# Gate and up units of both feed-forward blocks as seven half-width block products, a first part kept as it was

## What is computed

```
h = h + 0.5 * swiglu(rmsnorm_2(h, ffn1_norm), ffn1_w_gate, ffn1_w_up, ffn1_w_down)     # 528 tokens
... latent attention and delta net ...
h = h + 0.5 * swiglu(rmsnorm_2(h, ffn2_norm), ffn2_w_gate, ffn2_w_up, ffn2_w_down)     # only 512 are needed
def swiglu(x, w_gate, w_up, w_down): return (silu(x @ w_gate) * (x @ w_up)) @ w_down   # 1024 -> 2816 -> 1024
```

## Time and profile before

| | |
|---|---|
| median of 3 runs | 2112.35 us (2111.82 to 2117.05) |
| span of the profiled execution | 2111.5 us; the profile gives no time beside the span |
| block 1 (window 797 to 1178.9) | from its unit 1 to the last down product |
| block 2 (window 1740 to 2098.3) | the same |
| TensorE busy | 2059.4 us, 98% |
| Vector, Scalar, GpSimd busy | 817.3, 736.1, 761.0 us |

### The profile page before, as it was taken

One profiled execution on the slowest core, in us unless ns is written; L12 is line 12 of the kernel. 1 busy time (PEld: TensorE's weight loads), 2 busy tenths in 40 slices (PEclk: granted clock), 3 DMA queues, 4 the chain that ended last, 5 costly groups with the idle time before them and its releaser, 6 DMA issues.

```text
span 2111.5 us, 32172 instructions
## 1 busy us (share of the span) xinstructions
PE 2059.4 (98%) x13992; PEld 1769.5 (84%) x13992; DVE 817.3 (39%) x1300; ACT 736.1 (35%) x1140; POOL 761.0 (36%) x243
## 2 busy tenths in 40 slices
PE   8999999999999999999999999999999999999998
PEld 6899888878977789999999878798777788888886
DVE  4400675145357655220222242266566644211222
ACT  5332222336556544221222344342312323222222
POOL 4433232545310054334333431045243235434432
PEclk9999999999999999999999999999999999999999
DMA  5323122222310122223323431222013223223322
GB/s 173 100 87 109 52 74 80 80 90 81 100 61 21 41 80 81 81 75 106 100 66 94 103 100 31 60 68 81 22 62 111 81 82 98 90 83 107 100 68 72
DMA packets 170052, 171.52 MB, mean 81 GB/s; under 512 B 16940, under 2 KB 160680, under 8 KB 169912
## 3 DMA queue, kind: packets, MB, share of 16 engines
q1 hardware_dynamic: 168508, 167.25, 25.1%
q10 hardware_dynamic: 1404, 2.23, 0.3%
HBM read 163.17 MB, written 6.29 MB: 80 GB/s over the span
## 4 chain that ended last, share of the span: by engine, by line
PE 89%; DVE 4%; issue 3%; ACT 2%; POOL 1%; DMA 1%; ACTq 0%; SPq 0%; DVEq 0%; POOLq 0%
PE ps L2101 87%; PE ps L2103 2%; DMA x_rows<-in_x 0%; ACT diag L927 0%; DVE gdn_x L1966 0%; DVE gdn_inv_t L1949 0%; POOL w_lo L758 0%; POOL stat L775 0%; ACT u_hi L953 0%; DMA ret_decay<-c_decay 0%; ACT w_hi L899 0%; ACT residual L952 0%; DVE gdn_inv_t L1945 0%; DVE tmp L1414 0%; DVE sg L1609 0%
## 5 line engine op out<-in xcount | busy, mean ns | idle before, releaser
L758 POOL TENSOR_TENSOR w_lo<-w_raw,w_hi 128x2048 fp32r<-128x2048 f32 (+3 forms) x153 | 654.8, 4282 | 901.7 <-ACT w_hi L899 896.2
L2101 PE MATMUL ps<-u_hi,w_hi 128*128 128x512 f32 (+1 forms) x1904 | 584.4, 347 | 9.8 <-DVE sg L1609 2.6
L2101 PE MATMUL ps<-u_hi,w_lo 128*128 128x512 f32 (+1 forms) x1904 | 578.6, 344 | 0.0
L2101 PE MATMUL ps<-u_lo,w_hi 128*128 128x512 f32 (+1 forms) x1904 | 569.5, 344 | 1.0 <-DVE u_lo L1402 0.8
L2101 PEld LDWEIGHTS ps<-u_hi,w_hi 128*128 128x128 f32 x1904 | 328.6, 189 | 53.0 <-issue 5.5
L2101 PEld LDWEIGHTS ps<-u_lo,w_hi 128*128 128x128 f32 x1904 | 326.6, 189 | 43.7 <-DVE u_lo L1402 5.5
L2101 PEld LDWEIGHTS ps<-u_hi,w_lo 128*128 128x128 f32 x1904 | 328.1, 189 | 40.0 <-issue 0.5
L899 ACT ACTIVATE w_hi<-w_raw 128x2048 fp32r<-128x2048 f32 (+3 forms) x157 | 279.0, 1779 | 175.0 <-PE ps L2101 168.9
L2101 PE MATMUL ps<-hidden_hi,w_hi 128*128 128x264 f32 (+1 forms) x528 | 141.1, 321 | 0.0
L2101 PE MATMUL ps<-hidden_lo,w_hi 128*128 128x264 f32 (+1 forms) x528 | 141.0, 322 | 0.0
L2101 PE MATMUL ps<-hidden_hi,w_lo 128*128 128x264 f32 (+1 forms) x528 | 140.8, 321 | 0.0
(11 more groups left out here) (379 smaller groups left out, 2959.8 us busy)
## 6 DMA issues: line engine op xcount, KB each, us to landing
w_raw<-in_w_in_a SPq DMA_DIRECT2D x22, 1024.0 KB, 5.3
w_raw<-in_ffn_w_gate SPq DMA_DIRECT2D x22, 1024.0 KB, 5.4
w_raw<-in_ffn_w_up SPq DMA_DIRECT2D x22, 1024.0 KB, 5.4
w_raw<-in_w_in SPq DMA_DIRECT2D x17, 1024.0 KB, 5.2
w_raw<-in_ffn_w_down SPq DMA_DIRECT2D x16, 768.0 KB, 4.2
w_raw<-in_ffn_w_down SPq DMA_DIRECT2D x16, 640.0 KB, 3.9
w_raw<-in_w_out_a SPq DMA_DIRECT2D x8, 1024.0 KB, 5.0
w_raw<-in_w_kv SPq DMA_DIRECT2D x8, 1024.0 KB, 5.4
```

Source lines behind the costliest of these rows:

```text
L758: pool.tensor_tensor(WL[:, u % RAWS, part], RAW[:, u % RAWS, part], WH[:, u % SPLITS, part].bitcast(F32), ALU.subtract).then_inc(lo_done, 1)
L2101: return nc.tensor.matmul(o, a, b, start=start, stop=stop, **kw)
```

## The change

FFN_PARTS becomes (4, 6, 6, 6), and each part's down product has 4 units that hold all of the part's rows. The 4 gate and up units of the first part are computed as before. The 18 of the others are computed in blocks. Write a unit's weights as a 2 x 2 of blocks (4 row blocks of 128 by 128 columns, b11 to b22) and the input as a 2 x 2 (4 feature blocks by half of the tokens). Seven products p1 to p7 of blocks or of sums of blocks, 12 matmuls of 264 or 256 columns each, give the four output blocks. TensorE adds where it can: a product is accumulated into a bank that already holds another, seeded by a Scalar copy from bank to bank (y from p1, w from y behind p6), while p5 is copied to SBUF and added by Vector to y and, from w, to z. The banks: x, w are slot s0, y, z slot s1; at the end x|w and y|z are the two output chunks.

- The input is normalised once per block: Vector makes `normed` (8 operations of width 528 or 512) behind unit 0, its three sums behind unit 1, their low parts behind units 2 and 3; Scalar makes the high parts. During the first two down units u_hi and u_lo are rewritten from `normed`. Silu then reads PSUM directly.
- Weights: Vector makes four sums of 512 elements (one in place in RAW), and the low part of the first 1024 elements and of the 1536 of the sums; Scalar makes the high parts in three pieces; GpSimd makes the low part of the last 1024 only.
- All this is done one unit ahead, between the pieces for the current unit. The first unit of a part's sevens is prepared in the third down unit before it.
- For the first two seven-product units of each block TensorE starts banks y and w with one matmul each before the Scalar seeds.

The core of the diff (indentation cut by 8):

```diff
-FFN_PARTS = (12, 10)
+FFN_PARTS = (4, 6, 6, 6)
+ORDER = ("p1", "p5", "p6", "p2", "p7", "p3", "p4")
...
-    ffns[name] = [(job(part, spread_after=3 if name == "ffn1" and part == FFN_PARTS[0] else None),
-                   job(8, fold=2, kc=part // 2)) for part in FFN_PARTS]
+    ffns[name] = [(job(part, spread_after=3 if name == "ffn1" and n == 0 else None), job(4, kc=part))
+                  for n, part in enumerate(FFN_PARTS)]
...
+        if u in seven_no:
+            v = seven_no[u]
+            pool.wait_ge(w_summed, 4 * v + 4)
+            pool.wait_ge(sum_lo, 2 * v + 1)
+            lo_part(u, slice(UNIT // 2, UNIT), u + 2)
+        elif u < n_units:
...
+        if u + 1 in seven_no and u not in seven_no:
+            return
+        if u + 2 in seven_no:
+            first_rows_hi(u + 2)
+            last_rows_hi(u + 2)
+            summed_hi(u + 2)
+        else:
+            hi(u + 2)
...
+    def first_rows_hi(u):
+        v = seven_no[u]
+        a, b, half = u % RAWS, u % SPLITS, UNIT // 2
+        act.wait_ge(done, unit_ticks[u - SPLITS])
+        act.wait_ge(w_summed, 4 * v + 2)
+        nc.scalar.activation(WH[:, b, 0:half], RAW[:, a, 0:half], ACT.Copy).then_inc(sum_hi, 1)
+    def last_rows_hi(u):
+        hi_part(u, slice(UNIT // 2, UNIT), raw_in[u % RAWS])
+    def summed_hi(u):
+        v = seven_no[u]
+        if v >= 2:
+            act.wait_ge(done, unit_ticks[seven_units[v - 2]])
+        if u in first_sevens:
+            act.wait_ge(mixed, 10 * first_sevens.index(u) + 10)
+        act.wait_ge(w_summed, 4 * v + 4)
+        nc.scalar.activation(TH[:, v % 2, :], TF[:, v % 2, :], ACT.Copy).then_inc(sum_hi, 1)
...
+        def seven_unit(jg, i, j):
+            u = jg.unit0 + 4 * i + j
+            v = seven_no[u]
...
+            x, y, z, w = 2 * s0, 2 * s1, 2 * s1 + 1, 2 * s0 + 1
+            act.wait_ge(prod, product_tick(u, "p1"))
+            nc.scalar.activation(PS[:, y, 0:half], PS[:, x, 0:half], ACT.Copy).then_inc(seeded, 1)
+            act.wait_ge(prod, product_tick(u, "p5"))
+            if v:
+                act.wait_ge(added, 2 * v)
+            nc.scalar.activation(P5[:, 0:half], PS[:, z, 0:half], ACT.Copy).then_inc(seeded, 1)
+            if u + 1 in seven_no:
+                first_rows_hi(u + 1)
+            act.wait_ge(prod, product_tick(u, "p6"))
+            nc.scalar.activation(PS[:, w, 0:half], PS[:, y, 0:half], ACT.Copy).then_inc(seeded, 1)
+            if u + 1 in seven_no:
+                last_rows_hi(u + 1)
+                summed_hi(u + 1)
+            if u + 2 not in seven_no:
+                hi(u + 2)
+            for m in (1, 0):
+                slot, uses = slots[m]
+                if j % 2 == 0:
+                    if m:
+                        act.wait_ge(prod, product_tick(u, "p3"))
+                        act.wait_ge(added, 2 * v + 2)
+                    else:
+                        act.wait_ge(done, unit_ticks[u])
+                    nc.scalar.activation(SG[:, m, 0:width].rearrange("p (a n) -> p a n", a=2),
+                                         PS[:, 2 * slot:2 * slot + 2, 0:half], ACT.Silu).then_inc(ps_free[slot], 1)
+                else:
+                    act.wait_ge(ps_free[slot], uses + 1)
+                    nc.scalar.activation(HH[:, 4 * i + 2 * (j // 2) + m, 0:width], TMP[:, m, 0:width], ACT.Copy).then_inc(hh_done, 1)
...
+    def w_sums(u):
+        if u not in seven_no:
+            return
+        v = seven_no[u]
+        e, a = v % 2, u % RAWS
...
+        dve.wait_ge(raw_in[a], 16 * (u // RAWS + 1) + 16 * extra_loads(u))
+        if v >= 2:
+            dve.wait_ge(done, unit_ticks[seven_units[v - 2]])
+        nc.vector.tensor_tensor(t3, b12, b22, ALU.subtract).then_inc(w_summed, 1)
+        dve.wait_ge(w_summed, 4 * v + 1)
+        nc.vector.tensor_tensor(b12, b12, b11, ALU.subtract).then_inc(w_summed, 1)
+        dve.wait_ge(w_summed, 4 * v + 2)
+        nc.vector.tensor_tensor(t2, b12, b22, ALU.subtract).then_inc(w_summed, 1)
+        dve.wait_ge(w_summed, 4 * v + 3)
+        nc.vector.tensor_tensor(t4, b21, t2, ALU.add).then_inc(w_summed, 1)
+    def first_rows_lo(u):
+        v = seven_no[u]
+        a, b, half = u % RAWS, u % SPLITS, UNIT // 2
+        dve.wait_ge(sum_hi, 2 * v + 1)
+        dve.wait_ge(w_summed, 4 * v + 3)
+        nc.vector.tensor_tensor(WL[:, a, 0:half], RAW[:, a, 0:half], WH[:, b, 0:half].bitcast(F32),
+                                ALU.subtract).then_inc(sum_lo, 1)
+    def summed_lo(u):
+        v = seven_no[u]
+        dve.wait_ge(sum_hi, 2 * v + 2)
+        nc.vector.tensor_tensor(TL[:, v % 2, :], TF[:, v % 2, :], TH[:, v % 2, :].bitcast(F32),
+                                ALU.subtract).then_inc(sum_lo, 1)
...
+    def normalise(name, number):
         cols = norms[name][1]
         width = width_of(cols)
+        for k in range(KC):
+            last = nc.vector.scalar_tensor_tensor(out=UN[:, k, 0:width], in0=RES[:, k, cols], scalar=gain(name, k),
+                                                  in1=RSTDB[:, 0:width], op0=ALU.mult, op1=ALU.mult)
+        last.then_inc(mixed, 1)
...
+        dve.wait_ge(mixed, 10 * number + 1)
+        nc.vector.tensor_tensor(s3, a21, a11, ALU.subtract).then_inc(mixed, 1)
+        dve.wait_ge(mixed, 10 * number + 2)
+        nc.vector.tensor_tensor(a21, a21, a22, ALU.add).then_inc(mixed, 1)
+        dve.wait_ge(mixed, 10 * number + 3)
+        nc.vector.tensor_tensor(s2, a11, a21, ALU.subtract).then_inc(mixed, 1)
+        dve.wait_ge(mixed, 10 * number + 4)
+        nc.vector.tensor_tensor(s4, a12, s2, ALU.add).then_inc(mixed, 1)
...
+            if j == 0:
+                normalise(name, number)
+            if j == 1:
+                mix_sums(name, number)
+            if j == 2:
+                mix_low(1, 1)
+                mix_low(0, 2)
+            if j == 3:
+                mix_low(2, 3)
...
+        def seven_unit(part, jg, i, j):
+            u = jg.unit0 + 4 * i + j
+            v = seven_no[u]
+            slots = [chunk_of(jg, i, j, m) for m in range(2)]
+            (s0, uses0), (s1, uses1) = slots
+            y, z, w = [PS[:, b, 0:half] for b in (2 * s1, 2 * s1 + 1, 2 * s0 + 1)]
+            up = j % 2
+            def hidden_out(m):
+                slot, uses = slots[m]
+                gate_slot, gate_uses = chunk_of(jg, i, j - 1, m)
+                dve.wait_ge(ps_free[gate_slot], gate_uses + 1)
+                nc.vector.tensor_tensor(TMP[:, m, 0:width].rearrange("p (a n) -> p a n", a=2),
+                                        SG[:, m, 0:width].rearrange("p (a n) -> p a n", a=2),
+                                        PS[:, 2 * slot:2 * slot + 2, 0:half], ALU.mult).then_inc(ps_free[slot], 1)
+            w_sums(u + 1)
+            dve.wait_ge(prod, product_tick(u, "p6"))
+            dve.wait_ge(seeded, 3 * v + 3)
+            nc.vector.tensor_tensor(y, P5[:, 0:half], y, ALU.add).then_inc(added, 1)
+            if u + 1 in seven_no:
+                first_rows_lo(u + 1)
+            dve.wait_ge(prod, product_tick(u, "p7"))
+            nc.vector.tensor_tensor(z, P5[:, 0:half], w, ALU.add).then_inc(added, 1)
+            if up:
+                dve.wait_ge(prod, product_tick(u, "p3"))
+                dve.wait_ge(added, 2 * v + 2)
+                hidden_out(1)
+            elif (i, j) != (0, 0):
+                tile = 2 * i + j // 2 - 1
+                for m in range(2):
+                    hidden_low(part, tile, m, 2 * tile + 2)
+            if u + 1 in seven_no:
+                summed_lo(u + 1)
+            if up:
+                dve.wait_ge(done, unit_ticks[u])
+                hidden_out(0)
...
+                if part == 0 and j < 2:
+                    rows = slice(k4 * j, k4 * (j + 1))
+                    dve.wait_ge(mix_hi, 5 * number + 4 + j)
+                    nc.vector.tensor_tensor(UL[:, rows, cols], UN[:, rows, 0:width], UH[:, rows, cols].bitcast(F32),
+                                            ALU.subtract).then_inc(mixed, 1)
...
+    def seven(name, number, jb, n, cols):
+        i, j = n // 4, n % 4
+        u = jb.unit0 + n
+        v, half, k4 = seven_no[u], width_of(cols) // 2, KC // 2
+        a, b, e = u % RAWS, u % SPLITS, v % 2
+        (s0, uses0), (s1, uses1) = [chunk_of(jb, i, j, m) for m in range(2)]
+        x, y, z, w = 2 * s0, 2 * s1, 2 * s1 + 1, 2 * s0 + 1
+        low, high = slice(cols.start, cols.start + half), slice(cols.start + half, cols.stop)
...
+        made = {"p1": (own(0, 0), plain(0, low), x, True), "p5": (own(0, 1), plain(0, high), z, True),
+                "p6": (summed(0), mixed_in(0), y, False), "p2": (own(1, 0), plain(k4, low), x, False),
+                "p7": (summed(1), mixed_in(1), w, False), "p3": (own(1, 1), mixed_in(2), y, False),
+                "p4": (summed(2), plain(k4, high), w, False)}
+        for name in ORDER:
+            if name == "p1":
+                pe.wait_ge(sum_lo, 2 * v + 1)
+                if u in first_sevens:
```

(77 more changed lines are left out.)

187 lines of the change are left out of this document (123 added, 64 removed).

## The result

The changed kernel takes 2090.53 us (median of 4 runs, 2087.86 to 2090.91); the kernel before took 2114.7 beside it (4 runs). The ratio is 0.9883, 95% interval 0.9867 to 0.9899: faster by 1.2%. The forecast was 2096.5 with its own range from 2086 to 2107. The profiled execution spans 2088.5 us against 2111.5.

The account below looks back on a forecast made before the run. TensorE, busy 98% of the span, was taken as the bound, so matmul columns set the cost. Terms of -21.5 and +5.6 for the clock took 2111.5 to a 2095.6 span, median 2096.5; own range 2086 to 2107, with rivals 2072 to 2113.

Parts of the forecast that it names:

- The columns, -47.5: Gate and up units of both blocks: 84 half-width matmuls instead of 96 in 18 units each, 47.5 us less.
- The last seven-product unit, +13.8: Last such unit per part: GpSimd's split delays Vector's sums' low part, p6 waits 2.2 or 2.4, six times, +13.8 us.
- Twelve short waits, +2.4: Gate units behind up units: Scalar's seed ready at 3.0, p6 wants it at 2.9; 0.2 each, +2.4 us.
- Block 1's first part, +4.4: Vector's eight normalising operations after unit 0 delay unit 2's second chunk: +4.4 us, 0 to 9.
- Block 2's first part, +4.2: Normalising plus GpSimd splits make a hidden low part late for the first down product: +4.2 us, 0 to 7.
- Clock, +5.6: Eight new waits in dense feed-forward work may lower TensorE's granted clock, 0.7 us each: +5.6 us.
- Rival A: The port does not stop Vector long, or Scalar's copy comes 1.5 later: 2074 us, chance 0.12.
- Rival B: Vector is the bound in every unit, 11.1 us a unit: 2109 us, chance 0.12.
- Rival C: The clock falls after each wait of p6 and of the first parts: slower, 2122 us, chance 0.12.
- First sums, low parts and rewriting in the first down units, 0: Block 1's first down units: 25.9 us of Vector work against 23.5 of down units, costing 0, up to 2.
- start matmuls: Matmuls into two banks for four units, 8 of 264 or 256 columns: +1.0 us.

Follow-up runs that it names:

- e6: Changed kernel with e2's order, plus normalise behind unit 1 and all three low parts of the input sums behind unit 3: 2067.01 us, 0.9782.
- e2: Changed kernel with Vector making the low part of the next unit's weight sums ahead of the hidden low parts in gate units: 2075.41 us, 0.982.
- e5: Changed kernel with Scalar's high part of the coming down unit later only in a part's second last seven-product unit: 2075.93 us, 0.9825.
- e7: Changed kernel with GpSimd's 1536-element low part of a down unit split into three instructions of 512: 2084.1 us, 0.9863.
- e8: e2 with two more Vector sums of 384 elements in every preparation of a seven-product unit: 2075.47 us, 0.9824.
- e1: Changed kernel with Scalar's high part of the coming down unit later in both last seven-product units of a part: 2121.56 us, 1.0038.
- e4: Kernel before with parts (4, 6, 6, 6) and undivided down units, all gate and up units full products: 2114.36 us, 0.9999.
- e3: Changed kernel with Vector's normalising moved from behind unit 0 to behind unit 1's hidden low parts: 2090.28 us, 0.9885.

## Why the prediction was right, and where it was off

- **The columns, -47.5.** Right. e6 has no new wait in the blocks; its span is 48.1 us shorter than before, of which 1.6 are clock loss (6.1 - 4.5). That leaves 46.5, where 47.5 - 1.0 were booked. In the changed kernel two units together take 20.55 us in block 1 (p6 starts at 888.74 and 909.29) and 19.87 in block 2 (1799.70 and 1819.57), where twice 10.28 and twice 9.95 were booked.
- **The last seven-product unit, +13.8.** Right in place, number and size: six waits, 13.0 in all, 2.0 and 2.3 where 2.2 and 2.4 were forecast. The walk gave 13.1 us from the start of the gate unit to the end of GpSimd's split, 13.7 to the end of the second hidden low part and 15.5 to that of the sums' low part. That unit starts at 906.35 (worked out in the next item), and the three end at 919.47, 920.03 and 921.71: 13.1, 13.7 and 15.4. The mechanism is shown by three separate edits. Doing the wanted operation first (e2) and letting the split loose later (e5) remove the waits whole; shorter pieces (e7) halve them. By the Trainium skill, "SBUF — State Buffer", section "Who interferes with whom", the loser is blocked for the whole instruction. The trace agrees: in e5 GpSimd takes 4.29 instead of 3.51 when Vector came first. That the two take turns when both queue stands on e7.
- **Twelve short waits, +2.4.** Wrong: none appears. The rows of one such unit of block 1:

```profile
887.58 0.65 ACT L1242 ACTIVATE hidden_hi<-tmp 128x528 fp32r<-128x528 f32 x1 [1.63 <-DVE tmp L1885]
888.13 0.38 ACT L1216 ACTIVATE ps<-ps 128x264 f32<-128x264 f32 x1
...
888.74 0.28 PE L2353 MATMUL ps<-mix_hi,w_sum_hi 128*128 128x264 f32 x1
```

TensorE starts p6 at 888.74, so the unit began 24 matmuls of 0.1224 earlier, at 885.80. (The next gate unit, which the item above uses, begins two units later, 20.55, at 906.35.) Scalar begins the seed at 888.13 and ends it at 888.51, 2.7 after the unit's start, not 3.0. Instructions on one engine begin up to 0.1 before the one ahead has ended, and over the chain that saved 0.3 us, more than the whole term. In all twelve units the seed is ready 0.16 to 0.24 us early; the waits were missed by that much. With more work for Vector (e8) three of them do appear.
- **Block 1's first part, +4.4.** Measured 2.0. Two terms were off. Eight normalising operations take 5.52 back to back, not 6.1, for the same overlap. And the clock fell at 808 to 812, ahead of any new wait; it slowed TensorE by some 1.7 us, so that it came late by itself. Where the fall comes later, as in e1 and e8, the same wait is 3.5. So the small 2.0 is luck in part: e4 has the fall at 808 as well, without the change in the products.
- **Block 2's first part, +4.2.** Measured 2.8, at the first down unit as forecast. The normalising with one split inside took 9.77 us where 10.7 (6.1 and 4.6) were booked, and the rest of a walk of 30 us was another half a microsecond too long. The row of the normalising:

```profile
1735.68 9.77 DVE L1809 SCALAR_TENSOR_TENSOR normed<-residual,gains,rstd_row 128x512 f32<-128x512 f32 x8
```

e6 shows that only the order made these waits. e3 shows that half the order is not enough.
- **Clock, +5.6.** The sum is close (11.2 - 6.1 = 5.1), by luck in part. Eight waits were measured, and two of them, at 1763.9 and 1841.9, had a low clock behind them, some 1.7 us each: 3.4. The other 1.7 is what is left of falls that stand behind no new wait: two came, at 808 and 1644, and the one at 722 went away. The forecast wanted a low clock only behind the new waits, and that is wrong. The fall at 808 begins as the wait of 1.6 us that the kernel before has too ends, and e4 trades 722 for 808 in the same way. What makes a fall come at 722, 808 or 824 in one kernel or another, and at 1644, stays open.
- **Rival A** (the port does not stop Vector) is out by the six waits. In e5, which is its second condition, and in e2 the time is its time: 2074 named, 2075.9 and 2075.4 measured. That is luck in part: the rival took off 4.2 for block 2's first part, whose 2.7 or 2.8 both kernels still have, and left in the 2.4 of short waits that never came. **Rival B** (Vector bound in every unit) is out by the list of waits, which has none in every unit, and by e8: 1.1 us more a unit cost three waits of 0.4. **Rival C** did not happen in the changed kernel. It is no fancy, though: in e1, where two waits of 2.2 to 2.9 stand 4 us apart at the end of each part, the clock fell six times out of six and the kernel came out slower than before. That its 2121.56 is C's 2122 is chance: e1 has 36.9 us of waits where C had 25.0, and 21.3 us more clock loss than before where C had 31.6.
- **First sums, low parts and rewriting in the first down units, 0.** Right: no wait for `u_lo` or `mix_lo` is in the list.

The span came out 7.1 us below the 2095.6 forecast: the terms for short waits (2.4), first parts (4.0), last units (0.8) and clock (0.5) were together 7.7 too high. The median stands 2.0 above the span, not 0.85, which makes the error of the forecast 6.0. (In each of the changed kernel's four runs time and span lie 1.9 to 2.1 apart; the 0.85 set the median of some runs against the span of another.) Against the kernel before as it ran beside, 2114.7, the gain is 24.2, where the forecast had 2112.35 - 2096.5 = 15.9.

## What to carry to other kernels

When Vector gets more work with both inputs in SBUF beside GpSimd's splits, do not ask only whether the busy times fit: look for the place where a long GpSimd instruction is let loose just ahead of the one Vector operation that TensorE wants next. The cure cost nothing here: put the wanted operation first, or release the split later. Before moving a release, walk through *every* unit that shares the line, since the split goes somewhere: in e1 it landed on worse ground and turned 1.2% faster into 0.4% slower. The rest of the gain was in the column count: 84 against 96 half-width matmuls gave the 47.5 us that it promised, less 1.0 for the start matmuls, once the waits were gone.

## What was not expected of the hardware

- Turns at the port are by instruction: a queued Vector operation of 0.70 us with both inputs in SBUF is held up by the GpSimd instruction that is ahead, 1.28 us long in e7, 3.5 in the changed kernel, and in both it gets the next turn even while GpSimd has more queued.
- In e2 the port stops Vector in every gate unit (the low part of the sums takes 2.9 to 3.0 there instead of 1.75), and TensorE does not wait for it once. In e8 it takes 2.9 to 3.4.
- Of the waits of 2.0 to 2.3 us alone in dense work, three of twelve had a fall of the granted clock to its lower level (1.2 GHz) within 1 us of their end (one of six in the changed kernel, two of six in e3), and none of the six of 0.9 to 1.2 in e7 had. The wait of 2.5 to 2.8 in block 2's first part had one in each of the seven kernels that have it. The pairs of e1 had one each time (six of six), but four of the six falls begin with the end of the first wait, 2.6 to 2.7 long; that it takes a pair is not shown.
- A Scalar copy from bank to bank in PSUM of 264 elements took 0.375 us, and a Vector addition of 264 from SBUF and PSUM 0.44, where the prediction had 0.4 and 0.42 from other forms.
